# Two large mixers of a one-core kernel: the gated levels of linear attention packed into two runs of small matmuls, selections on diagonal blocks, a softplus gate

## The reference

```python
h = rmsnorm(x, attn_norm_g[l])
(cq, ckv, krope, cb, cc, cx, dq, dk, dv, iq, ik, iw,
 gq, gk, gv, glr, gr, gate_pre) = jnp.split(h @ w_in[l], split_points, axis=-1)
branches = (mla, conv, dsa, gla)                       # four branches of width 256
merged = sum of sigmoid(gate_pre)[n] * (branches[n] @ w_branch[l, n])
x = x + merged @ w_out[l]

# dsa: an indexer scores every key for every query, the top 64 keys are attended
rel = relu(einsum('bqhd,bsd->bqhs', q_idx, ik) * 32 ** -0.5)      # 8 index heads of 32
score = einsum('bqh,bqhs->bqs', w * 8 ** -0.5, rel)               # then causal, top_k

# gla: gated linear attention, 4 heads, key width 32, value width 64, chunks of 64 tokens
log_alpha = log_sigmoid(glr @ w_gate_up + b_gate) / 16
cum  = cumsum of log_alpha within a chunk
attn = einsum('bhik,bhjk,bhijk->bhij', qc, kc, exp(cum_i - cum_j)) for j <= i
o = (qc * exp(cum)) @ state + attn @ vc
state = exp(last) * state + (kc * exp(last - cum))^T @ vc
o = rmsnorm(o, norm_g);  out = silu(gr) * o

# mla: two low-rank projections, each after an rmsnorm, then causal attention
q = rmsnorm(cq, q_norm_g) @ w_q_up;  kv = rmsnorm(ckv, kv_norm_g) @ w_kv_up
```

## Time and profile before

| | |
|---|---|
| median of 3 runs | 1790.62 us |
| the profiled execution | 1790.6 us |
| its span | 1788.8 us |
| instructions | 24871 |
| TensorE (PE) busy | 1773.4 us, 99% |
| VectorE (DVE) busy | 1265.8 us, 71% |
| ScalarE (ACT) busy | 949.3 us, 53% |
| DMA | 309.24 MB, 173 GB/s mean |
| granted TensorE clock | 0.999 of full speed |

### The profile page before, as it was taken

One profiled execution on the slowest core, in us unless ns is written; L12 is line 12 of the kernel. 1 busy time (PEld: TensorE's weight loads), 2 busy tenths in 40 slices (PEclk: granted clock), 3 DMA queues, 4 the chain that ended last, 5 costly groups with the idle time before them and its releaser, 6 DMA issues.

```text
span 1788.8 us, 24871 instructions
## 1 busy us (share of the span) xinstructions
PE 1773.4 (99%) x9702; PEld 1509.7 (84%) x9702; DVE 1265.8 (71%) x1893; ACT 949.3 (53%) x1348; POOL 30.2 (2%) x39
## 2 busy tenths in 40 slices
PE   9999999999999999999999999999999999999998
PEld 8888888888888888888888788888888878888887
DVE  7774795776577657677656877777755778677774
ACT  6554655554555546555545535455545544555553
POOL 0000000000000001000000000000000000000000
PEclk9999999999999999999999999999999999999999
DMA  8666523666666555366655534556655443456652
GB/s 274 191 179 202 175 72 110 193 180 199 177 195 184 198 170 189 108 198 183 196 175 180 180 125 132 179 178 189 190 196 171 140 156 127 151 187 192 190 195 108
DMA packets 227677, 309.24 MB, mean 173 GB/s; under 512 B 22558, under 2 KB 176318, under 8 KB 227562
## 3 DMA queue, kind: packets, MB, share of 16 engines
q1 hardware_dynamic: 227398, 307.35, 54.8%
q10 hardware_dynamic: 164, 0.30, 0.0%
HBM read 306.57 MB, written 1.05 MB: 172 GB/s over the span
## 4 chain that ended last, share of the span: by engine, by line
PE 91%; DVE 5%; ACT 2%; issue 1%; SPq 0%; DMA 0%; POOL 0%; POOLq 0%; ACTq 0%; DVEq 0%
PE ps L645 26%; PE ps L596 15%; PE ps L598 15%; PE ps L597 15%; PE ps L647 13%; DVE wlo L1737 1%; PE ps L1141 1%; PE ps L608 1%; PE ps L816 1%; PE ps L842 1%; DVE ev_acc L1746 1%; ACT whi L1239 1%; PE ps L829 1%; PE ps L784 0%; DVE m_scr L1746 0%
## 5 line engine op out<-in xcount | busy, mean ns | idle before, releaser
L1737 DVE TENSOR_TENSOR wlo<-staging,whi 128x1024 fp32r<-128x1024 f32 (+1 forms) x580 | 692.4, 1210 | 338.6 <-ACT whi L1239 338.5
L1239 ACT ACTIVATE whi<-staging 128x1024 fp32r<-128x1024 f32 (+1 forms) x580 | 607.3, 1051 | 475.2 <-PE ps L598 293.0
L645 PE MATMUL ps<-hT,whi 128*128 128x512 f32 x1984 | 624.0, 396 | 0.1
L647 PEld LDWEIGHTS ps<-hT,wlo 128*128 128x128 f32 x1984 | 372.7, 188 | 88.1
L647 PE MATMUL ps<-hT,wlo 128*128 128x256 f32 x1984 | 389.8, 278 | 0.0
L645 PEld LDWEIGHTS ps<-hT,whi 128*128 128x128 f32 x1984 | 302.0, 189 | 0.4 <-DVE wlo L1737 0.3
L596 PE MATMUL ps<-whi,fh 128*128 128x512 f32 x504 | 196.1, 389 | 0.0
L597 PE MATMUL ps<-wlo,fh 128*128 128x512 f32 x504 | 196.1, 389 | 0.0
L598 PE MATMUL ps<-whi,fl 128*128 128x512 f32 x504 | 196.1, 389 | 0.0
L596 PE MATMUL ps<-whi,hT 128*128 128x512 f32 (+3 forms) x464 | 184.7, 398 | 0.8 <-DVE wlo L1737 0.6
L598 PE MATMUL ps<-whi,hT 128*128 128x512 f32 (+3 forms) x464 | 177.4, 382 | 0.0
(11 more groups left out here) (347 smaller groups left out, 1904.4 us busy)
## 6 DMA issues: line engine op xcount, KB each, us to landing
staging<-in_w_in SPq DMA_DIRECT2D x92, 512.0 KB, 3.4
staging<-in_ffn_w_gate SPq DMA_DIRECT2D x84, 512.0 KB, 4.3
staging<-in_ffn_w_up SPq DMA_DIRECT2D x84, 512.0 KB, 4.5
staging<-in_ffn_w_down SPq DMA_DIRECT2D x84, 512.0 KB, 4.0
staging<-in_w_ffn_gate SPq DMA_DIRECT2D x44, 512.0 KB, 4.5
staging<-in_w_ffn_up SPq DMA_DIRECT2D x44, 512.0 KB, 4.6
staging<-in_w_ffn_down SPq DMA_DIRECT2D x44, 512.0 KB, 4.3
staging<-in_od_w_in SPq DMA_DIRECT2D x16, 512.0 KB, 3.7
```

Source lines behind the costliest of these rows:

```text
L645: e.matmul(o, wh[:, kk, j * 128:j * 128 + 128], hT[:, k, :], start=k == 0, stop=False)
L647: m = e.matmul(o[:, 0:256], wl[:, kk, j * 128:j * 128 + 128], hTh[:, k, :], start=False, stop=k == KD - 1)
L1239: e.activation(high(u)[:, 0:n], stage[u % NS][:, 0:n], ACT.Copy).then_inc(*K.inc("hi", ("hi", u)))
L1737: e.tensor_tensor(low_of(u)[:, 0:n], stage[u % NS][:, 0:n], high(u)[:, 0:n].bitcast(F32), ALU.subtract).then_inc(*K.inc("lo", ("lo", u)))
```

## The change

All of it is in mixer m0 and m1.

**Levels.** The seven runs of TensorE become two: levels 0 to 3 in round 22, levels 4 to 6 in round 27. A level is now computed only on the diagonal blocks of 64 by 64 tokens: 16 matmuls of 32 rows by 64 columns by 64 (four blocks of tokens, four heads). A head has a bank of its own, and a level its 128 columns in it, 64 for each 128 tokens; the first and second 64 of those 128 tokens go to the first and second 64 partitions of the bank. The wait between halves is gone. `kl` and `ql` have four buffers.

**Selections.** The masks are 64 columns wide. DVE copies 128 x 256 (two heads) at a time into a new tile `near`, which lies over `e2` and `kd` and is set to zero by POOL, and ACT copies `near` into `gat` in two parts at the end (two instructions).

```diff
-                    for lev in range(7):
-                        yield
-                        kk, qq = (m.gk, m.gq) if lev == 0 else (m.kl[lev % 2], m.ql[lev % 2])
-                        ps = [room((P, "lev", lev, x)) for x in range(2)]
...
-                        for half in range(2):
-                            if half:
-                                e.wait_ge(*K.at(P, "lev mm", lev, 0))
...
+                    for some in (range(0, 4), range(4, 7)):
+                        for _ in range(4):
+                            yield
+                        if some[0]:
+                            yield
+                            for h in range(4):
+                                done(P, "lev", 0, h)
+                        ps = [b for h in (0, 2) for b in room_two((P, "lev", some[0], h), (P, "lev", some[0], h + 1))]
+                        if some[0] == 0:
                             e.wait_ge(*K.at("ev", (P, "gqk")))
+                        e.wait_ge(*K.at(P, "ql", some[-1]))
+                        for lev in some:
+                            kk, qq = (m.gk, m.gq) if lev == 0 else (m.kl[lev % 4], m.ql[lev % 4])
                             for t in range(2):
+                                c = 128 * (lev % 4) + 64 * t
+                                for h in range(4):
+                                    for half in range(2):
+                                        sl = slice(t * 128 + 64 * half, t * 128 + 64 * half + 64)
+                                        w = e.matmul(ps[h][64 * half:64 * half + 64, c:c + 64], kk[32 * h:32 * h + 32, sl],
+                                                     qq[32 * h:32 * h + 32, sl], start=True, stop=True)
...
+                    for made, begun, kept in ((0, 1, ()), (1, 2, ()), (2, 3, ()), (3, 0, ()), (0, 4, ()), (4, 5, (0,)),
+                                              (5, 0, (1,)), (0, 6, (2,)), (6, 0, (3,)), (0, 0, ()), (0, 0, (4, 5, 6))):
+                        if made:
+                            scaled(made)
+                        if begun:
+                            decays(begun)
+                        for lev in kept:
+                            gathered(lev)
+                        yield
```

```diff
-                        for h0 in (0, 2):
-                            ps = room_pair((P, "idx", t, h0), (P, "idx", t, h0 + 1))
...
+                        ps = [b for h0 in (0, 2) for b in room_two((P, "idx", t, h0), (P, "idx", t, h0 + 1))]
...
+                            for x in range(4):
+                                rows = slice(32 * x, 32 * x + 32)
...
+                    ps = [room((P, "st", x)) for x in range(2)]
+                    e.wait_ge(*K.at("ev", (P, "kd")))
                     for c in range(3):
```

```diff
-                    e.activation(m.e1[:, :], m.e1[:, :], ACT.Exp, scale=-1.0).then_inc(*K.inc("gla_act"))
-                    e.wait_ge(*K.now("gla_act"))
-                    e.activation(m.e1[:, :], m.e1[:, :], ACT.Ln, bias=1.0).then_inc(*K.inc("gla_act", (P, "ln")))
+                    e.wait_ge(*K.at(P, "gup mm"))
+                    e.wait_ge(*K.at(P, "less gbg"))
+                    e.activation(m.e1[:, :], bk(P, "gup")[:, 0:256], ACT.Softplus, scale=-1.0,
+                                 bias=m.gbg[:, 0:1]).then_inc(*K.inc("gla_act", (P, "softplus"), ("ev", (P, "gup"))))
```

**Mla and order.** The scaling of `cq` and `ckv` by their rstd (four DVE operations) moves into the copies out of PSUM, half of which go from DVE to ACT. The output norm of gla takes both 128-token halves in one operation. On DVE the due splits stand first in rounds 18 to 26 of the gla branch's turn and, on DVE and ACT, first in each round from 27 on:

```diff
-                weave([(1, gates()), (30, short_conv()), (1, dsa()), (5, gla()), (27, mla()), (TURN[0], turn()),
-                       (33, conv_low())], catch_up)
+                weave([(1, gates()), (27, lows(25)), (30, short_conv()), (1, dsa()), (18, lows(9)), (5, gla()),
+                       (27, mla()), (TURN[0], turn()), (33, conv_low())], catch_up)
```

More of the change, by code:

```diff
@@ L176, in take_pair, with take_two @@
         return b, before
+    def take_two(self, one, two):
+        at = {b: n for n, b in enumerate(self.free)}
+        beside = [(b, b + 1) for b in at if b + 1 in at]
+        pair = min(beside, key=lambda p: max(at[p[0]], at[p[1]])) if beside else tuple(self.free[0:2])
+        before = []
+        for c, user in zip(pair, (one, two)):
+            self.free.remove(c)
+            self.of[user] = c
+            before.append(self.had.get(c))
+            self.had[c] = user
+        return pair, before
     def give(self, b):
@@ L576, in room_pair, with room_two @@
                 return PS[:, b, :], PS[:, b + 1, :]
+            def room_two(one, two_):
+                pair, before = B.take_two(one, two_)
+                for user in before:
+                    if user is not None:
+                        e.wait_ge(*K.at("ev", user))
+                return [PS[:, b, :] for b in pair]
             def done(*user):
@@ L1062, in dsa @@
                         nk = 128 * (t + 1)
[L1063 to L1075 removed]
+                        ps = [b for h0 in (0, 2) for b in room_two((P, "idx", t, h0), (P, "idx", t, h0 + 1))]
+                        if t == 0:
+                            e.wait_ge(*K.at(P + "ik T", 0))
+                        for j in range(2):
+                            for x in range(4):
+                                rows = slice(32 * x, 32 * x + 32)
+                                w = e.matmul(ps[x][:, j * nk:(j + 1) * nk], m.iqT[rows, j, t * 128:t * 128 + 128],
+                                             m.ikT[rows, 0, 0:nk], start=True, stop=True)
+                        w.then_inc(*K.inc("att", (P, "idx mm", t)))
+                        for x in range(4):
+                            done(P, "idx", t, x)
+                        yield
+                        yield
                         for _ in range(5):
@@ L1147, in gla @@
+                        w.then_inc(*K.inc("gla_mm", (P, "lev mm", some[0])))
+                    yield
+                    yield
+                    for h in range(4):
+                        done(P, "lev", 4, h)
+                    yield
                     for t in range(2):
@@ L1170, in mla @@
                     two_ps = [room((P, "cq", q)) for q in range(2)]
-                    e.wait_ge(*K.at(P, "c scaled"))
+                    for t in range(2):
+                        e.wait_ge(*K.at("in ev", g, X2[3][0], t))
                     for k in range(3):
```

239 lines of the change are left out of this document (123 added, 116 removed).

## The result

The kernel after takes 1800.45 us (median of 4 runs, 1798.56 to 1802.88) against 1791.12 us before, a ratio of 1.0052 with a 95% interval of 1.0041 to 1.0064. Forecast were 1772.6 us and a range up to 1785. The profiled execution took 1799.37 us with a span of 1797.6.

The account below looks back on a forecast made before the run. TensorE, busy 99% of the span, was taken as the bound. For each mixer 7.4 + 2.0 + 1.4 + 0.3 + 0.5 - 2.3 - 0.3 = 9.0 us, so 1790.6 - 18.0 = 1772.6 us; 8-in-10 range 1765.5 to 1785.

Parts of the forecast that it names:

- Levels: Seven level runs costing 11.45 us become two costing 4.05, four tiles at a time: gain 7.4 us for each mixer.
- The serial rival: At the two level runs, each pass costs a fixed 0.061 us by itself: slower, 1796.5 us; chance 0.09.
- Indexer: One run of eight matmuls replaces two for each 128 queries, as long as one now: gain 2.0 us per mixer.
- state: One run of three matmuls, 1.2 us, replaces three runs of one, 2.6 us: gain 1.4 us per mixer.
- up-projection: With 128 rows, same mode as its neighbours, passes stay and edges go: gain 0.3 us per mixer.
- the stall behind the Ln: At the gate, Softplus removes DVE's Ln wait and TensorE's later wait for a split: gain 0.5 us per mixer.
- The wait of the run of 48: Packed run of levels 4 to 6 waits for level 6's scaled queries and DVE's last earlier selection: 2.3 us per mixer.
- The wait of the run of 64: Packed run of levels 0 to 3 waits for level 3's queries, behind dsa scores and two splits: 0.3 us per mixer.
- 0.8 of scores, 2.4 of two splits and 0.7 of scaling: DVE's chain to level 3's queries after L842: 4.65 us in all, against 4.35 that TensorE needs.
- the later waits ... have 1 to 2.4 us to spare and I cost them at nothing: Output matmuls waiting for `gat` and mla's copies cost nothing; 1 us if ACT's copies come one split later.
- no gain: Rival: the change's runs take two at a time at 0.11 us, levels lose 1.95: 1791.3 us; chance 0.06.
- the forecast's gross gain: Shortening of TensorE's program before waits: levels 7.4, indexer 2.0, state 1.4, up-projection 0.3, gate 0.5; 11.6 us per mixer.

Follow-up runs that it names:

- the second experiment: Kernel after without the rule that due splits stand first on DVE in rounds 18 to 26: 1785.70 us, ratio 0.9964 to the kernel before.
- the fastest kernel: Kernel after, splits first in no round, second half of gate 2 ahead of branch 1's products, run of levels 0 to 3 one round later: 1767.23 us.
- the filling matmuls: Kernel after plus 146 matmuls with overwritten results in TensorE's idle times, needing only the bank that is free early (second attempt): 1790.49 us, ratio 1.0005.
- rope: Kernel after with mla's twelve rope operations on DVE two rounds later, behind the short convolution's last operation: 1793.07 us, ratio 1.0017.
- gate order: Kernel after with the second half of gate 2 ahead of the two products of branch 1: 1786.12 us, ratio 0.9975.
- the rule from round 27: Due splits stand first in each round from 27 on, on DVE and ACT; kernel after without this rule: 1793.88 us, ratio 1.0020.
- four edits of the order: Kernel after without splits first in rounds 18 to 26 or from 27, gate 2's second half earlier, levels 0 to 3 a round later: 1767.23 us.

## Why the prediction was wrong

**Levels: right mechanism, two sizes off that nearly cancel.** 4.05 us were forecast for the two runs that come. In the second experiment they put 1.51 and 1.18 us between their start and the next weight matmul, and with the edges about 3.0. What goes was put at 11.5, seven times 1.64. By the starts of the kernel before and of the fastest kernel, in m0, five of the seven runs cost 1.6 us and two, which stand between other small matmuls, 1.42: 10.8. The gain is 7.8 us where 7.4 were forecast, and that it is so near is in part luck. 128 passes start in 1.37 us, 0.085 for eight of them. Whether eight tiles go at once at 0.085 or four at 0.043 isn't told apart by any run. The serial rival (0.061 a pass, 7.8 us) is out. The Trainium skill, "TensorEngine Tiling (Array Packing)", section Tiling Modes, says that tiles of different rows and columns work in parallel; the trace agrees, at least for four row groups, by the indexer's run below.

**Indexer, state, up-projection: right but for a small wait.** A run of eight 32-row matmuls now has 0.66 us to the next weight matmul where four had 0.65:

```profile
968.01 0.73 PE L1097 MATMUL ps<-m_scr 32*128 32x128 f32 x16
968.67 0.46 PE L624 MATMUL ps<-whi,hT 128*128 128x416 f32 x1
```

By the starts the indexer gave 1.4 us (2.0 forecast; a new wait of 0.4 us at L1118 is in it), the state 1.4 (1.4), the up-projection 0.4 (0.3), and the stall behind the Ln is gone, 0.6 (0.5). With the 7.8 of the levels that is 11.6 us, as forecast; as what is left over in the result it was 10.9 and 11.6.

**The wait of the run of 48: right.** 2.3 us forecast, 2.38 and 2.71 measured, by the chain that the earlier trace rows show:

```profile
1045.94 0.69 DVE L1994 TENSOR_TENSOR m_bl<-ps,m_bh 128x512 fp32r<-128x512 f32 x1 [1.57 <-ACT m_bh L1395]
1046.89 2.36 DVE L1789 TENSOR_TENSOR wlo<-staging,whi 128x1024 fp32r<-128x1024 f32 x2 [0.26 <-ACT whi L1274]
1049.50 0.42 DVE L2521 TENSOR_TENSOR m_scr<-m_scr 128x256 f32<-128x256 f32 x1
1049.84 0.76 DVE L2539 COPY_PREDICATED m_scr<-cst,ps 128x256 f32<-128x256 int32 x2
```

**The wait of the run of 64: mis-sized.** 0.3 us were forecast, 2.64 and 2.80 measured. The step "0.8 of scores, 2.4 of two splits and 0.7 of scaling" laid DVE's operations end to end. In the trace both splits first wait for ACT, whose own splits stand behind other work of its order, the first behind the tanh of a gate (L1599), the second behind the exponentials of the dsa softmax (L1422):

```profile
1023.60 1.23 DVE L1789 TENSOR_TENSOR wlo<-staging,whi 128x1024 fp32r<-128x1024 f32 x1 [0.97 <-ACT whi L1274]
1025.79 1.23 DVE L1789 TENSOR_TENSOR wlo<-staging,whi 128x1024 fp32r<-128x1024 f32 x1 [0.97 <-ACT whi L1274]
1026.93 0.42 DVE L2520 TENSOR_TENSOR m_scr<-m_scr 128x256 f32<-128x256 f32 x1
1027.60 0.42 DVE L2045 TENSOR_TENSOR m_nat<-ps,m_scr 128x256 f32<-128x256 f32 x1
```

Twice 0.97 is most of the gap; the bank of the dsa output, free 0.3 us after the queries, is another part.

**The step that failed: "the later waits ... have 1 to 2.4 us to spare and I cost them at nothing".** The waits of gla and mla were looked at, the convolution's wasn't, since the change doesn't edit its steps. But TensorE's distance from the convolution's inputs to the first branch product became shorter, because the output matmuls of gla and the last levels, which lay in between, now stand earlier: by the starts 3.0 and 1.2 us less of TensorE lie between the two in m0. The kernel before, at this place:

```profile
1081.49 1.23 DVE L1737 TENSOR_TENSOR wlo<-staging,whi 128x1024 fp32r<-128x1024 f32 x1 [1.83 <-ACT whi L1239]
1084.75 0.68 DVE L2347 TENSOR_TENSOR m_bl<-m_G,m_bh 128x512 fp32r<-128x512 f32 x1
1085.53 0.47 PE L596 MATMUL ps<-whi,m_bh 128*128 128x512 f32 x1
```

DVE ends the operand at 1085.43, TensorE starts at 1085.53 without a wait: nothing to spare, and no idle time on TensorE that would have said so. DVE itself had stood still for 1.8 us ahead of the split at 1081.49; ACT, which writes `whi`, had been waiting for TensorE's own matmuls of gla (L1158), among those that have moved. After, DVE works without a break of note from 1076.08 on, TensorE is there at about 1080.3, and both meet at 1085.53 again. The first and last operations of DVE's stretch after:

```profile
1076.08 1.23 DVE L1789 TENSOR_TENSOR wlo<-staging,whi 128x1024 fp32r<-128x1024 f32 x1 [2.84 <-ACT whi L1274]
1077.22 0.34 DVE L2383 TENSOR_SCALAR m_G<-m_G,m_cvw 128x256 f32<-128x256 f32 x1
...
1084.73 0.69 DVE L2399 TENSOR_TENSOR m_bl<-m_G,m_bh 128x512 fp32r<-128x512 f32 x1
```

5.2 us in each mixer, 10.4 in all, which rope, gate order and the rule from round 27 each changed by their own amount.

**Left out altogether: the clock.** No rival had TensorE's clock fall. It costs 4.0 and 7.4 us here, and of these 11.4 the filling matmuls brought back 8.5 by the starts in the mixers and 10.0 by the medians of two sessions. The forecast took an idle microsecond for a microsecond; with the half clock behind it, an idle time of 2.6 us or more nearly always lost another 1.7 or 3.4 us, of which up to 1 us fell into the idling itself. The Trainium skill, "TensorE: Matmul & The Clock Gate", section HAM oscillation, describes such waits between bursts of matmuls, there for DMA and 3 to 5 us long, that bring the engine back to its lower clock. The trace agrees on that, and here waits of 2.6 to 2.8 us for DVE were followed by it too.

A slip in one rival, without weight for the forecast: 112 steps of 0.11 are 12.3 us and not 12.5, which moves "no gain" from 1791.3 to 1790.9.

With the forecast's gross gain, the measured waits and the clock: 11.6 - 10.2 - 4.0 = -2.6 in m0 and 11.6 - 10.7 - 7.4 = -6.5 in m1, 9.1 us slower in all, against 9.3 measured.

## What to carry to other kernels

When a change shortens the in-order program of the engine that bounds a kernel, list every wait behind it on that engine, the ones whose code isn't edited too, and find for each when its operand was ready before: one that was ready 0.1 us ahead of its use shows no idle time, and the 5.2 us came there. In this kernel an idle time of TensorE of 2.6 us or more had to be costed at its length and 1.7 or 3.4 us for the half clock behind it. When such a change comes out slower, look at the gross gain first: here 11 us in each mixer were really there, and four edits of the order, none of them of the computation, turned 1800.4 us into 1767.2.

## What the runs showed of the hardware that was not expected

- Idle times of TensorE in the mixers of seven profiled executions (the kernel after and six experiments): of 0.8 to 1.4 us none was followed by half clock; of 2.33 to 2.38 us three of six; of 2.60 to 2.80 us 16 of 17; of 3.0 to 5.2 us all six. What was lost then (missing clock summed over the stretch) was each time 1.7 or 3.4 us, for idle times of the same length as well.
- Half clock stretches the packed small matmuls less than the large ones: the run of 48 takes 1.70 us from its start to the next weight matmul instead of 1.18, weight matmuls of 512 columns go from 0.23 to 0.43 us apart.
- Four 32-row tiles cost no more than two: 0.66 us for eight matmuls in four row groups, 0.65 for four in two.
